# A decoder step with 32 experts: one engine loop for experts 8 to 27, and the last down matrix in four transfers

## The reference

```python
def moe_ffn(h, router_w, router_b, w_up, b_up, w_down, b_down):
    logits = (x2d @ router_w + router_b).astype(jnp.float32)
    top_val, top_idx = lax.top_k(logits, TOP_K)          # 4 of 32
    gate = jax.nn.softmax(top_val, axis=-1)
    ...
        u = xblk @ w_up[e] + b_up[e]
        glu, lin = jnp.split(u, 2, axis=-1)
        ...
        return act @ w_down[e] + b_down[e]
    ...
x = x + g2 * moe_ffn(h, ...)
y_prompt = rms_norm(yp, final_norm_g)
```

## Time and profile before

| | |
|---|---|
| median of 3 runs | 1141.28 us (1140.9 to 1141.94) |
| the profiled execution | 1141.32 us, its span 1139.6 us, mean granted clock 0.991 |
| TensorE busy | 1098.8 us (96%), weight loads 495.0 us (43%) |
| VectorE, ScalarE, GpSimd busy | 416.2 us (37%), 187.0 us (16%), 25.0 us (2%) |
| DMA | 460.42 MB, 404 GB/s over the span |
| last chain | TensorE 77%, DMA 20% |

### The profile page before, as it was taken

How to read it: one execution, slowest core, us unless ns; L and a number is a source line. 1 busy time by engine, 2 the same in 40 slices (tenths; PEclk the granted TensorE clock), 3 DMA queues, 4 the chain that set the end, 5 groups by cost and what they waited for, 6 DMA issues and landing times.

```text
span 1139.6 us, 14866 instructions
## 1 busy us (share of the span) xinstructions
PE 1098.8 (96%) x6104; PEld 495.0 (43%) x6104; DVE 416.2 (37%) x871; ACT 187.0 (16%) x383; POOL 25.0 (2%) x57
## 2 busy tenths in 40 slices
PE   7999999999999999999999998999999999999996
PEld 5767678743334333333333333333333333333333
DVE  3157654343333333333323334333333333333333
ACT  1252223211111111111101011111111111111112
POOL 1100100000000000000000000000000000000002
PEclk9999999999999999999999998999999999999998
DMA  9988959999999999999999999999999999999993
GB/s 377 417 330 321 363 198 377 362 397 414 430 400 428 428 426 434 433 430 433 428 431 432 429 434 430 433 429 434 430 428 435 426 436 428 435 429 426 428 427 156
DMA packets 33529, 460.42 MB, mean 404 GB/s; under 512 B 5088, under 2 KB 6112, under 8 KB 12096
## 3 DMA queue, kind: packets, MB, share of 16 engines
q1 hardware_dynamic: 27808, 448.33, 93.2%
q0 software_dynamic: 2688, 9.47, 2.4%
q10 hardware_dynamic: 2976, 1.81, 0.5%
HBM read 454.94 MB, written 4.65 MB: 403 GB/s over the span
## 4 chain that ended last, share of the span: by engine, by line
PE 77%; DMA 20%; DVE 1%; issue 0%; ACT 0%; POOL 0%; DVEq 0%; SPq 0%; ACTq 0%
PE bank L1494 32%; PE bank L1550 15%; DMA ring<-in_w_up 13%; PE bank L1108 7%; PE bank L1537 5%; PE bank L1467 4%; DMA ring<-in_w_last 3%; PE bank L1362 3%; PE bank L1514 3%; DMA ring<-in_w_ada 1%; PE bank L1476 1%; DMA arena<-sample_values 1%; PE bank L1069 1%; PE bank L1525 1%; PE bank L1704 1%; DMA sample_values<-ring 1%
## 5 line engine op out<-in xcount | busy, mean ns | idle before, releaser
L1494 PE MATMUL bank<-ring,arena 128*64 128x512 f32 x2016 | 449.6, 598 | 14.4 <-DMA ring<-in_w_up 14.3
L1494 PEld LDWEIGHTS bank<-ring,arena 128*64 128x64 f32 x2016 | 141.5, 138 | 310.6 <-issue 286.2
L1550 PE MATMUL bank<-ring,arena 128*64 128x512 f32 x960 | 212.7, 595 | 0.0
L1550 PEld LDWEIGHTS bank<-ring,arena 128*64 128x64 f32 x960 | 66.6, 137 | 124.7 <-issue 123.8
L1108 PE MATMUL bank<-arena,ring 128*128 128x264 f32 x448 | 106.4, 391 | 0.7 <-DVE arena L1813 0.7
L2196 DVE COPY arena<-bank 128x512 f32<-128x512 f32 x32 | 22.1, 692 | 191.2 <-PE bank L1494 191.2
L918 ACT ACTIVATE arena<-bank 128x512 f32<-128x512 f32 x32 | 19.2, 599 | 435.5 <-PE bank L1494 435.5
L1108 PEld LDWEIGHTS bank<-arena,ring 128*128 128x128 f32 x448 | 82.8, 190 | 17.7 <-issue 4.3
L2250 DVE TENSOR_TENSOR arena<-bank,arena 128x512 f32<-128x512 f32 x31 | 21.4, 692 | 187.4 <-PE bank L1550 187.4
L1537 PE MATMUL bank<-arena,gpickT 64*128 64x512 f32 x240 | 76.7, 628 | 0.0
L2245 DVE TENSOR_TENSOR arena<-arena,bank 128x512 f32<-128x512 f32 x120 | 74.2, 680 | 0.0
(11 more groups left out here) (348 smaller groups left out, 691.6 us busy)
## 6 DMA issues: line engine op xcount, KB each, us to landing
ring<-in_w_up SPq DMA_DIRECT2D x41, 4096.0 KB, 29.0
ring<-in_w_up SPq DMA_DIRECT2D x43, 2048.0 KB, 14.3
ring<-in_w_down SPq DMA_DIRECT2D x21, 4096.0 KB, 26.7
ring<-in_w_down SPq DMA_DIRECT2D x18, 2048.0 KB, 13.1
ring<-in_w_ada SPq DMA_DIRECT2D x24, 1024.0 KB, 9.7
ring<-in_w_in SPq DMA_DIRECT2D x12, 1024.0 KB, 11.7
ring<-in_w_o SPq DMA_DIRECT2D x4, 1024.0 KB, 9.8
arena<-in_w_up SPq DMA_DIRECT2D x5, 512.0 KB, 19.7
```

What stands on the lines that cost most here:

```text
L1494: last = mm(bank[64 * half:64 * half + 64, b, :], xe[:, par, k % 4, k // 4, :], src[:, 512 * half:512 * half + 512], start=(k == 0), stop= ...
L1550: last = mm(bank[64 * half:64 * half + 64, b, :], acts[:, k, :], src[:, 512 * half:512 * half + 512], start=(k == 0), stop=(k == KT - 1))
```

## The change

The second loop and the straight experts between the loops go: `experts` now has experts 0 to 7, one loop with five rounds for 8 to 27, and 28 and 29 behind it. `MIDDLE_AT` becomes 28, since the block of biases needs a straight expert. `LAST_COLS` has four pieces of 128 columns, the fourth in bank 2 like the second; both halves of `w_last` come as two transfers of 1 MiB, with the semaphore `half_in` for the second.

```diff
-LAST_COLS, LAST_BANK = ((0, 256), (256, 384), (384, 512)), (3, 2, 5)
+LAST_COLS, LAST_BANK = ((0, 128), (128, 256), (256, 384), (384, 512)), (3, 2, 5, 2)
...
-MIDDLE_AT = 16
-LOOPS = (MIDDLE_AT - PEEL) // UNROLL
-LATE = 2
+MIDDLE_AT = 28
+LOOPS = (NE - 2 - PEEL) // UNROLL
...
     with eng.Fori(0, LOOPS) as q:
         for r in range(PEEL, PEEL + UNROLL):
             yield q * UNROLL + r, r, q
-    for n in range(MIDDLE_AT, MIDDLE_AT + UNROLL):
-        yield n, n, 0
-    with eng.Fori(0, LATE) as q:
-        for r in range(MIDDLE_AT + UNROLL, MIDDLE_AT + 2 * UNROLL):
-            yield q * UNROLL + r, r, q
-    for n in range(MIDDLE_AT + UNROLL + LATE * UNROLL, NE - 2):
+    for n in range(PEEL + LOOPS * UNROLL, NE - 2):
         yield n, n, 0
...
+            for s, second in enumerate(("half_in", "parts_in")):
+                i = last_load(*LAST[s - 2])
+                reuse(i)
+                for half, name in enumerate((f"pair{expert_slot(i)}", second)):
+                    c0 = 2048 * half
+                    sp.dma_start(pairs[:, expert_slot(i), c0:c0 + 2048], a["w_last"][:, 4096 * s + c0:4096 * s + c0 + 2048]
+                                 ).then_inc(sem(name), 16)
...
-            pool.wait_ge(sem("junk_ready"), 2)
+            pool.wait_ge(sem("junk_ready"), 3)
...
-                n, i = c1 - c0, last_load(NE - 1, "down", min(m, 1))
+                n, i = c1 - c0, last_load(NE - 1, "down", m // 2)
...
-                src = pairs[:, slot, 2048:4096] if m == 2 else pairs[:, slot, 0:2 * KT * n]
+                src = pairs[:, slot, 2048 * (m % 2):2048 * (m % 2) + 2048]
...
+                if m == 3:
+                    pe.wait_ge(sem("junk_ready"), 2)
+                if m % 2 == 0:
+                    pe.wait_ge(sem(f"pair{slot}"), rounds)
                 else:
-                    pe.wait_ge(sem(f"pair{slot}"), rounds)
+                    pe.wait_ge(sem("half_in" if m == 1 else "parts_in"), 48)
...
-            down_last(1)
-            for m in range(2):
+            for m in range(3):
+                if m < 2:
+                    down_last(m + 1)
                 pe.wait_ge(sem("ysl_ready"), m + 1)
                 combine_into(gpickT_last, ysb_last, *LAST_COLS[m], False)
-            down_last(2)
-            pe.wait_ge(sem("junk_ready"), 1)
-            combine_into(gpickT, ysb, *LAST_COLS[2], True)
-            pe.wait_ge(sem("ysl_ready"), 3)
-            combine_into(gpickT_last, ysb_last, *LAST_COLS[2], False)
+            down_last(3)
+            combine_into(gpickT, ysb, *LAST_COLS[3], True)
+            pe.wait_ge(sem("ysl_ready"), 4)
+            combine_into(gpickT_last, ysb_last, *LAST_COLS[3], False)
```

More of the change, by code:

```diff
@@ L1698, in down_last @@
                     pe.wait_ge(sem("acc_s_used"), NE - 1)
-                    pe.wait_ge(sem("parts_in"), 48)
+                if m == 3:
+                    pe.wait_ge(sem("junk_ready"), 2)
+                if m % 2 == 0:
+                    pe.wait_ge(sem(f"pair{slot}"), rounds)
                 else:
-                    pe.wait_ge(sem(f"pair{slot}"), rounds)
+                    pe.wait_ge(sem("half_in" if m == 1 else "parts_in"), 48)
                 for k in range(KT):
@@ L1705, in down_last @@
                                   src[:, (2 * k + half) * n:(2 * k + half + 1) * n], start=(k == 0), stop=(k == KT - 1))
-                last.then_inc(sem("down_done" if m == 2 else "last_psum"), 1)
+                last.then_inc(sem("down_done" if m == 3 else "last_psum"), 1)
             def combine_into(gT, y, c0, c1, first):
@@ L1745, in _ @@
                         pe.wait_ge(sem("sum_used"), 4)
-                        pe.wait_ge(sem("junk_ready"), 3)
+                        pe.wait_ge(sem("junk_ready"), 4)
                         gather(n, first_blocks=False)
@@ L2341, in _ @@
             dve.wait_ge(sem("down_done"), NE)
-            take_last(2)
+            take_last(3)
             for i in range(2):
@@ L2345, in _ @@
             dve.wait_ge(sem("ys_ready"), 1)
-            dve.wait_ge(sem("junk_ready"), 3)
+            dve.wait_ge(sem("junk_ready"), 4)
             TT(ys[:, EARLY:], ys[:, EARLY:], junk_s[:, EARLY:], ALU.add).then_inc(sem("ys_ready"), 1)
```

## The result

The changed kernel takes 1151.12 us (median of 6 runs, 1150.27 to 1153.77) against 1141.73 for the kernel before in the same series (6 runs, 1140.9 to 1143.71): ratio 1.0082, 95% interval 1.0069 to 1.0096. It is slower by 9.4 us; 1152.7 was forecast.

A forecast was written before the change was run, and what follows sets the result against it. The weight stream was taken to bound from 585.73 us unless TensorE had fallen behind, with TensorE following closely at the end. Span 1139.6 + 14.8 - 2.2 + 0.3 - 1.5 = 1151.0, plus 1.7: 1152.7 us, range 1150.2 to 1155.9.

The forecast's parts named there:

- The stream bounds up to expert 27, TensorE after it: Experts 16 to 27: TensorE waits once per expert, restarts 29.14 us apart; after the block, no wait for a load.
- The block enters 28 for 14.8 us: Block of biases in expert 28, at 1044.19 us: adds 14.8 us to TensorE's queue, bounds 12.3 and 16.5.
- 2.2 us of slack behind it: After the block in expert 28: TensorE's remaining waits for loads, 0.88 and 1.34, take up 2.2 us of it.
- Expert 16 gives back 1.5 for the stream: Block leaves expert 16: the weight stream returns to 29.14 us per expert, saving 1.5 us, bounds 0 and 1.6.
- Loop rounds cost 0: Experts 16 to 27 join the loop: same instructions per expert, jumps back covered, cost 0.
- the sum: Whole kernel: 1139.6 + 14.8 - 2.2 + 0.3 - 1.5 = 1151.0 us of span, forecast time 1152.7; 78 in 100.
- Four pieces cost 0.3: w_last in the tail: narrower products and combines cost TensorE 0.3 us together.
- Hidden here too: Rival, from 1044 us on: the stream ends last, so the block at 28 costs nothing; 1138.8 us, 5 in 100.
- Already paid for at 16: Rival: catching up after expert 16 cost the stream as much as the block; about 1140.3 us, 3 in 100.
- Slower than the sum: Rival: lower TensorE clock after the block, or no stream gain; 1154.4 or 1154.2, both 1155.9 us; 14 in 100.

## Why the prediction was right, point by point

- **The stream bounds up to expert 27, TensorE after it.** Right: 16 restarts 29.14 apart, then no wait for a load behind the block. The first w_last product started at 1128.67, forecast was 1128.4.
- **The block enters 28 for 14.8 us.** The mechanism was right; the size was 16.0 in this execution and 14.8 (1057.71 - 1042.90) in the one with three pieces. The granted clock in the block's window was 0.69, and 0.77 before. It is a matter of the execution and not of the place: at 16 the block took 14.8, 15.8 and 14.6 us in three kernels, at 28 it took 16.0, 16.0, 14.8 and 15.9 in four. This term stayed inside its bounds, 12.3 to 16.5.
- **2.2 us of slack behind it.** 2.7 were measured. I counted the two waits with a bracket, and small waits inside rows came on top: from 1078.52 to 1086.49 the kernel before needed 7.97 us where the same work now takes 6.87, so 1.10 and not 0.88; from 1108.81 to 1117.34 it needed 8.53 where it now takes 6.92, so 1.61 and not 1.34.
- **Expert 16 gives back 1.5 for the stream.** The stream was 2.0 us ahead at the end, 0.4 of it already at the first restart. So the size was right, but by luck, since the reason that I gave, a shorter backlog while TensorE catches up, was wrong: the kernel with the block at 28 and the old loops lost the same 1.5 us in experts 20 and 21, where TensorE had not fallen behind at all. It is the long loop that gives the 1.5 us back. Between 600 and 1022 us the DMA view of the kernel before has `q8 instruction: 8` and `q14 instruction: 3`, loads of 16 and 8 KB of code for experts that run for the first time; the changed kernel, in its loop, has none. Eleven such loads are only 0.4 us of the stream by their bytes. But each is one packet, and a load of weights lands in 16 parts, the last of which counts. Loads of 4096 KB land 9.71 us apart. In the kernel with the block at 28 and the old loops two come later than that, by 0.35 and 1.17 us. In each case the first of the 16 parts is in time, the last one is not, and an instruction load of 16 KB, which takes 1.1 us, has started 3 to 5 us before (at 816.75 and 848.27). The kernel before has one such step of 1.39 us (instruction load at 893.58), the one with the block at 20 one of 1.55 (929.22). Most instruction loads cause no step, but among these four kernels no step of over 0.2 us comes without one, and in the changed kernel the loads land evenly. So code loading holds up one part of the stream, at a DMA share of 1.00.
- **Loop rounds cost 0.** The jumps cost nothing: in the changed kernel the restarts over three of the four jumps back are as far apart as those within a round, and at the first one (563.08) TensorE does not wait. What the sum lacked is that the long loop, with no code to load, is itself the source of the 1.5 us above.
- **Four pieces cost 0.3.** 0.4 was measured.
- **Not foreseen:** the pause that went, -1.7. The span came out 1.4 us below the sum: -0.5 for the stream, +1.2 for the block, -0.5 for the slack, +0.1 for the pieces, -1.7 for the pause. That the sum came so near is in part luck: +1.2 and the two -0.5 nearly cancel.
- **The rivals.** Hidden here too: refuted by the result, and by the 12 products behind 28, which were paid in full. The rule that stood behind it (the Trainium skill, Perfetto Trace Analysis, Identifying the Most-Contended Engine) names DMA as the engine to look at. Here DMA ran at its limit to the end of the stream, yet 9.4 us were lost on TensorE. Already paid for at 16: refuted by the result as well, and by the places 20 and 15, where the block costs nothing. Slower than the sum: the clock behind the block was normal, 7.09 for the 32 matmuls at 1058.61.

A version that beats both kernels came out of it: the four pieces, and the block in a straight expert between 11 and 20. With it at 15 the time is 1138.82 us, 0.31% below before (0.18 to 0.44), and with it at 20 it is 1138.94. Of these 3.2 us some 1.7 are the pause that is gone, which nobody placed on purpose and another edit may bring back; the rest fits the wait for w_last (1.6 us, less 0.4 for the narrow pieces).

## What to carry to other kernels

When two engines run at nearly the same pace, ask of a piece of work not which engine is the busier, but where in the program it stands: it is free if the steps behind it give the delay back (here 2.1 us per expert, so eight experts for a block of 16), and if the engine that it delays does not starve the other meanwhile (here no slot of the ring came free during the block, so the next load, due 7.4 us plus the block after the one before, had to be issued before that one landed). Both can be read from the trace before anything is moved: the distance of the restarts against the work in between, and the time from a load's issue to its landing at the place in question. Near the end of a kernel there is no slack left to give, so one-time work belongs in the middle.

## What the runs showed that I had not expected

- A pause of 2 us on the critical chain that comes and goes with edits elsewhere in the program (1.97, 1.96 and 2.44 us in three kernels, absent in ten), worth as much as the whole rearrangement of w_last. It ends 1.2 us after an instruction load.
- A stream of loads with a DMA share of 1.00 that is still 1.5 us slower over eight experts when their code runs for the first time, since an instruction load of 16 KB can hold up one of the 16 parts of a 4096 KB load by 1 us or more.
- The same 12 products took 10.57 us in one kernel and 12.16 in another behind the same block, at a granted clock of 1.00 and 0.86, and the block itself 14.6 to 16.0 us: the granted clock in and behind a stretch of short matmuls and waits differs from execution to execution.
